# Three row tiles of the first attention's output projection, with their norms, moved between the next tile's quads

## The reference, cut to what matters

```
h = rmsnorm(x, attn_pre_g)
proj = h @ w_in                     # queries, keys, values, gates
o_nsa = nsa_attention(...)          # 8 heads: compressed, selected and window branches
o_swa = swa_attention(...)          # 8 heads: window of 128 keys, with sinks
mix = concatenate([o_nsa, o_swa]) @ w_o
x = x + rmsnorm(mix, attn_post_g)
h = rmsnorm(x, mlp_pre_g)
gu = h @ w_gate_up                  # then the convolution, GELU, w_down
```

## Time and profile before

| | |
|---|---|
| median of three runs | 1631.01 us |
| the profiled execution's own time | 1629.0 us |
| its span in the trace | 1627.7 us |
| TensorE busy | 1505.7 us, 93% |
| VectorE, ScalarE, GpSimd busy | 69%, 38%, 44% |

### The profile page before, as it was taken

The page is one execution under the profiler, slowest core; times in us unless marked ns, Lnnn a source line. Parts: engine busy times, 40 slices in busy tenths (PEclk is TensorE's granted clock), DMA queues, the critical chain, the costliest instruction groups (busy, mean ns, idle before and its releaser), DMA issues.

```text
span 1627.7 us, 22505 instructions
## 1 busy us (share of the span) xinstructions
PE 1505.7 (93%) x8093; PEld 1291.1 (79%) x8093; DVE 1126.9 (69%) x2372; ACT 616.4 (38%) x1536; POOL 712.0 (44%) x668
## 2 busy tenths in 40 slices
PE   5998777999999999999999999999997999999997
PEld 4787455788888787877798899889885787899886
DVE  7746566457767769638867677767777588777764
ACT  3324556231221220113544554454455355344431
POOL 6855000347867748685444034303435114524430
PEclk8997799999999999999999999999999999999999
DMA  6622000424434336553311011101102321111121
GB/s 185 198 88 91 1 1 1 143 89 146 142 121 138 118 107 227 184 185 114 124 53 40 14 53 53 33 20 52 53 27 78 121 99 52 58 47 40 65 91 52
DMA packets 115887, 142.61 MB, mean 88 GB/s; under 512 B 11048, under 2 KB 75200, under 8 KB 115776
## 3 DMA queue, kind: packets, MB, share of 16 engines
q1 hardware_dynamic: 89968, 91.77, 18.2%
q10 hardware_dynamic: 25808, 49.40, 9.1%
HBM read 132.74 MB, written 8.40 MB: 87 GB/s over the span
## 4 chain that ended last, share of the span: by engine, by line
PE 65%; DVE 16%; ACT 8%; POOL 5%; issue 4%; DMA 1%; ACTq 0%; SPq 0%; DVEq 0%; POOLq 0%
PE ps L510 17%; PE ps L512 17%; PE ps L511 17%; POOL w_lo L499 3%; PE ps L1486 2%; PE ps L1290 2%; ACT p L2130 2%; POOL w_hi L497 2%; DVE st L2911 2%; PE ps L924 1%; PE ps L982 1%; PE ps L948 1%; DVE p L2579 1%; PE ps L1500 1%; PE ps L902 1%
## 5 line engine op out<-in xcount | busy, mean ns | idle before, releaser
L497 POOL TENSOR_SCALAR w_hi<-w_raw 128x512 fp32r<-128x512 f32 x308 | 236.5, 768 | 640.5 <-PE ps L512 484.9
L499 POOL TENSOR_TENSOR w_lo<-w_raw,w_hi 128x512 fp32r<-128x512 f32 x316 | 443.8, 1405 | 29.8 <-ACT w_hi L1676 4.1
L510 PE MATMUL ps<-w_hi,h_hi 128*128 128x384 f32 (+2 forms) x768 | 278.0, 362 | 8.1 <-POOL w_lo L499 2.9
L512 PE MATMUL ps<-w_hi,h_lo 128*128 128x384 f32 (+2 forms) x768 | 265.6, 346 | 0.0
L511 PE MATMUL ps<-w_lo,h_hi 128*128 128x384 f32 (+2 forms) x768 | 265.0, 345 | 0.0
L510 PE MATMUL ps<-h_hi,w_hi 128*128 128x512 f32 (+1 forms) x616 | 243.9, 396 | 6.3 <-DVE h_lo L2405 2.6
L512 PE MATMUL ps<-h_hi,w_lo 128*128 128x512 f32 (+1 forms) x616 | 236.7, 384 | 0.0
L511 PE MATMUL ps<-h_lo,w_hi 128*128 128x512 f32 (+1 forms) x616 | 236.5, 384 | 0.0
L2629 DVE SCALAR_TENSOR_TENSOR mod_acc<-mod_piece,csil,mod_acc 128x512 f32<-128x512 f32 x140 | 158.6, 1172 | 19.8 <-DMA mod_piece<-in_ada_w 16.0
L510 PEld LDWEIGHTS ps<-w_hi,h_hi 128*128 128x128 f32 x768 | 147.2, 192 | 20.4 <-POOL w_lo L499 4.3
L511 PEld LDWEIGHTS ps<-w_lo,h_hi 128*128 128x128 f32 x768 | 147.4, 192 | 8.3 <-issue 0.5
(11 more groups left out here) (337 smaller groups left out, 2999.4 us busy)
## 6 DMA issues: line engine op xcount, KB each, us to landing
mod_piece<-in_ada_w ACTq DMA_DIRECT2D x96, 256.0 KB, 3.0
w_raw<-in_w_gate_up SPq DMA_DIRECT2D x88, 256.0 KB, 3.1
w_raw<-in_a_w_in SPq DMA_DIRECT2D x128, 128.0 KB, 2.2
w_raw<-in_w_down SPq DMA_DIRECT2D x22, 512.0 KB, 4.5
w_raw<-in_b_w_in SPq DMA_DIRECT2D x20, 512.0 KB, 3.6
w_raw<-in_w_out SPq DMA_DIRECT2D x16, 512.0 KB, 3.9
w_raw<-in_w_in SPq DMA_DIRECT2D x8, 512.0 KB, 4.1
w_raw<-in_w_o SPq DMA_DIRECT2D x8, 512.0 KB, 3.9
```

The source lines that it names most:

```text
L497: pool.tensor_scalar(hi[:, e, :], raw[:, e, :], 1.0, 0.0, ALU.mult, ALU.add).then_inc(*s["pool_step"].up())
L499: m = pool.tensor_tensor(lo[:, e, :], raw[:, e, :], hi[:, e, :], ALU.subtract)
L510: pe.matmul(out, a[0], b[0], start=start, stop=False)
L512: return pe.matmul(out, a[1], b[0], start=False, stop=stop)
```

## The change

What is computed stays the same. The halves of the projection of tiles 0, 1 and 2 are cut into feature chunks of three matmuls and spread over steps of the next tile's quads (`O_STEPS`), all six of them into bank 3, one after the other. So the scores have three banks left, 0 to 2. ScalarE takes the squares of a finished half and copies it out of bank 3, behind the step after its last chunk. VectorE does the norm of a whole tile behind quads 12, 18 and 22 (`Y1_BEHIND`), ScalarE the squares of the summed rows of tiles 0 and 1 at steps 27 and 47. Tile 0's rows are turned at steps 47 and 51. After the quads are left: the turns of tiles 1 and 2, the projection and norms of tile 3, and the first half of the first gated product, now feature chunk by feature chunk over all four banks.

Two rules of the order change with it. Slots are scored to three behind the quad's last instead of four, but at least to the end of the next quad (`scored_behind`). Values are issued one pair at a time instead of two, and turned chunks have eight places instead of twelve. The rows `x2` and `y1` now lie where the queries of the same tile were, in pieces of 128 columns; their loads and stores move with them.

```diff
-SLOTS_T, SLOTS_T_EARLY = 12, 5
+SLOTS_T, SLOTS_T_EARLY = 8, 5
...
+    def x2(self, t):
+        return self.q_rows[:, 0:8, t * P:(t + 1) * P]
+    def y1(self, t):
+        return self.q_rows[:, 8:16, t * P:(t + 1) * P]
...
 def slots_behind(qs, n):
 
-    total = qs[-1].slots[-1] + 1
-    return range(0, 4) if n < 0 else [i + 4 for i in qs[n].slots if i + 4 < total]
+    if n < 0:
+        return range(0, SCORE_BANKS)
+    return range(scored_behind(qs, n - 1) + 1, scored_behind(qs, n) + 1)
+def scored_behind(qs, n):
+    last = qs[-1].slots[-1]
+    if n < 0:
+        return SCORE_BANKS - 1
+    if n + 1 == len(qs):
+        return last
+    return min(last, max(qs[n].slots[-1] + SCORE_BANKS, qs[n + 1].slots[-1]))
...
-VALUES_AT_ONCE = 2
+VALUES_AT_ONCE = 1
+SCORE_BANKS = 3
+O_STEPS = {(0, 0): range(12, 17), (0, 1): range(18, 23), (1, 0): range(27, 32), (1, 1): range(33, 39), (2, 0): range(45, 51), (2, 1): range(52, 58)}
+H2_STEPS = {47: (0, 0), 51: (0, 1)}
+X2_LOADS = {8: 0, 22: 1, 40: 2}
+ROW_SQUARES = {27: 0, 47: 1}
+Y1_BEHIND = {12: 0, 18: 1, 22: 2}
+H2_BEHIND = {19: (0, 0), 20: (0, 1)}
+def out_chunks(step):
+    parts = []
+    for (t, nh), steps in O_STEPS.items():
+        parts += [(t, nh, c) for c in range(KD) if steps[c * len(steps) // KD] == step]
+    return parts
+def halves_behind(step):
+    return [part for part, steps in O_STEPS.items() if steps[-1] + 1 == step]
...
-    if slot >= 4:
-        pe.wait_ge(*s["b_exped"].at(slot - 4))
+    if slot >= SCORE_BANKS:
+        pe.wait_ge(*s["b_exped"].at(slot - SCORE_BANKS))
...
-        out, x = k.ps[:, slot % 4, c0:c0 + q.w], k.qst[:, q.head0 + e, q.t * P:(q.t + 1) * P]
+        out, x = k.ps[:, slot % SCORE_BANKS, c0:c0 + q.w], k.qst[:, q.head0 + e, q.t * P:(q.t + 1) * P]
...
+    if first and q.kind == 2 and q.t == TX - 1:
+        pe.wait_ge(*s["turn_lo"].at(("h2", 0, 1)))
...
-            for part in values.pop(turn_number(qs, q.n, i), ()):
+            step = turn_number(qs, q.n, i)
+            for part in values.pop(step, ()):
                 pe_pair_values(k, pe, qs, *part)
+            for part in out_chunks(step):
+                pe_project_chunk(k, pe, *part)
+            if step in H2_STEPS:
+                pe_turn_rows(k, pe, *H2_STEPS[step], 7)
...
+def pe_project_chunk(k, pe, t, nh, c):
+    s = k.sig
+    if c == 0 and nh == 0:
+        pe.wait_ge(*s["o_lo"].at((t, 2)))
+    if c == 0 and t < TX - 1:
+        if nh == 1:
+            pe.wait_ge(*s["y_half"].at(("o", t, 0)))
+        elif t > 0:
+            pe.wait_ge(*s["y_half"].at(("o", t - 1, 1)))
+    if c == 0 and t == TX - 1:
+        if nh == 0:
+            pe.wait_ge(*s["b_exped"].at(quads()[-1].slots[-1]))
+        else:
+            pe.wait_ge(*s["y_half"].at(("o", t - 1, 1)))
+    if c % 2 == 0:
+        pe.wait_ge(*split_at(k, ("o", nh), c))
+    bank = 3 if t < TX - 1 else 2 + nh
+    m = three(pe, k.ps[:, bank, :], [x[:, c, t * P:(t + 1) * P] for x in k.h1], k.hl(("o", nh), c, 0, 512), c == 0, c == KD - 1)
+    if c == KD - 1:
+        m.then_inc(*s["prod"].up(("o", t, nh)))
+def pe_turn_rows(k, pe, t, g, bank):
+    s = k.sig
+    pe.wait_ge(*s["dve_step"].at(("out1", t)))
+    if (t, g) == (0, 1):
+        pe.wait_ge(*s["turn_lo"].at(("h2", 0, 0)))
+    if t == 1:
+        pe.wait_ge(*s["b_pt"].at(turn_number(quads(), len(quads()), 0) - 2 + g))
+    if t == 2:
+        pe.wait_ge(*s["o_lo"].at((TX - 1, 2)))
+    if t == 3:
+        pe.wait_ge(*s["turn_lo"].at(("h2", 2, g)))
+    for j in range(4):
+        m = pe.transpose(k.ps[:, bank, j * P:(j + 1) * P], k.y1(t)[:, 4 * g + j, :], k.ident[:, :])
+    m.then_inc(*s["turn_ps"].up(("h2", t, g)))
...
-    pe_first_cols(k, pe, 3, 0, range(FIRST_TURN_AT, KD))
+    for g in range(2):
+        pe_turn_rows(k, pe, 1, g, 4 + g)
+    for nh in range(2):
+        for c in range(KD):
+            pe_project_chunk(k, pe, TX - 1, nh, c)
+        if nh == 0:
+            for g in range(2):
+                pe_turn_rows(k, pe, 2, g, 6 + g)
+    pe.wait_ge(*k.sig["turn_lo"].at(("h2", 1, 1)))
+    for c in range(KD):
+        if c == FIRST_TURN_AT:
+            for g in range(2):
+                pe_turn_rows(k, pe, 3, g, 6 + g)
+        for i in range(4):
+            pe_first_cols(k, pe, i, 0, range(c, c + 1))
...
+            step = turn_number(qs, q.n, i)
+            for o in plan.pop(step, ()):
                 outputs(o)
+            if step == 1:
+                act.dma_start(k.post1[:, :], k.row(k.ins["attn_post_g"])).then_inc(*s["post1_in"].up("all", 16))
+            if step in X2_LOADS:
+                act_row_load(k, act, qs, X2_LOADS[step])
+            for part in halves_behind(step):
+                act_out_half(k, act, *part)
+            if step - 1 in H2_STEPS:
+                act_rows_turned(k, act, *H2_STEPS[step - 1], 7)
+            if step in ROW_SQUARES:
+                act_row_squares(k, act, ROW_SQUARES[step])
     for step in sorted(plan):
         for o in plan[step]:
             outputs(o)
+def act_row_load(k, act, qs, t):
+    s = k.sig
+    act.wait_ge(*s["b_scored"].at([q for q in qs if q.t == t and q.kind == 1][-1].slots[-1]))
+    act.dma_start(k.x2(t), k.xin()[:, t, :].rearrange("p (c n) -> p c n", n=P)).then_inc(*s[f"x2_in{t}"].up("x", 16))
+def act_out_half(k, act, t, nh):
+    s, half, out = k.sig, k.y1(t)[:, 4 * nh:4 * nh + 4, :], k.chunks(3)
+    act.wait_ge(*s["prod"].at(("o", t, nh)))
+    act.activation(half, out, ACT.Square, accum_out=k.halves[:, nh, 2 * t:2 * t + 1]).then_inc(*s["act_step"].up())
+    act.wait_ge(*s["act_step"].now())
+    act.activation(half, out, ACT.Copy).then_inc(*s["y_half"].up(("o", t, nh)))
+def act_rows_turned(k, act, t, g, bank):
+    act_turn(k, act, k.h1[0][:, 4 * g:4 * g + 4, t * P:(t + 1) * P], bank, ("h2", t, g), gain=k.gx[:, 1, 4 * g:4 * g + 4])
+def act_row_squares(k, act, t):
+    s = k.sig
+    act.wait_ge(*s["added"].at(("y1", t)))
+    act.dma_start(k.x_dram[:, t, :].rearrange("p (c n) -> p c n", n=P), k.x2(t)).then_inc(*s["x_out"].up(("1", t), 16))
+    act.activation(k.y1(t), k.x2(t), ACT.Square, accum_out=k.halves[:, 0, 2 * t + 3:2 * t + 4]).then_inc(*s["sq"].up(("y1", "x", t)))
...
-            if step <= turn_number(qs, q.n, 0):
+            if step <= turn_number(qs, q.n, len(q.chunks) - 1):
                 for o in plan.pop(step):
                     outputs(o)
+        if q.n in H2_BEHIND:
+            dve_rows_turned(k, dve, *H2_BEHIND[q.n], 7)
+        if q.n in Y1_BEHIND:
+            dve_add_out(k, dve, Y1_BEHIND[q.n])
...
+def dve_add_out(k, dve, t):
+    s, y, with_row = k.sig, k.y1(t), 0 < t < TX - 1
+    if t < TX - 1:
+        dve.wait_ge(*s["y_half"].at(("o", t, 1)))
+        first = k.halves[:, 0, 2 * t:2 * t + 1]
+        dve.tensor_tensor(first, first, k.halves[:, 1, 2 * t:2 * t + 1], ALU.add).then_inc(*s["dve_step"].up())
+        dve.wait_ge(*s["dve_step"].now())
+    else:
+        dve.wait_ge(*s["sq"].at(("y1", "y", t)))
+    if with_row:
+        dve.wait_ge(*s["sq"].at(("y1", "x", t - 1)))
+    dve_inverse_rms(k, dve, 2 * t, 2 * t + (2 if with_row else 1), ("y1", t))
+    dve.wait_ge(*s["rms"].at(("y1", t)))
+    if with_row:
+        dve_scale_out(k, dve, t - 1)
+    dve.wait_ge(*s["post1_in"].at("all"))
+    dve.wait_ge(*s[f"x2_in{t}"].at("x"))
+    gain = k.post1[:, :].rearrange("p (c n) -> p c n", n=P)
+    for nh in range(2):
+        half = slice(4 * nh, 4 * nh + 4)
+        x = y[:, half, :] if t < TX - 1 else k.chunks(2 + nh)
+        m = dve.scalar_tensor_tensor(y[:, half, :], x, k.stat[:, 1, 2 * t:2 * t + 1], gain[:, half, :], ALU.mult, ALU.mult)
+    m.then_inc(*s["dve_step"].up())
+    dve.wait_ge(*s["dve_step"].now())
+    dve.tensor_tensor(k.x2(t), k.x2(t), y, ALU.add).then_inc(*s["added"].up(("y1", t)))
```

More of the change, by code:

```diff
@@ L188, in lay_memory @@
         self.junk1 = Memory(nc, at_k).tile("junk1", [P, D])
-        late = Memory(nc, at_k)
-        self.x2, self.post1 = late.tile("x2", [P, TX, D]), late.tile("post1", [P, D])
-        assert late.offset <= m.offset
         after_k = m.offset
@@ L203, in lay_memory @@
         self.pt_early, self.pt_late = Memory(nc, at_acc).tile("pt_early", [P, SLOTS_T_EARLY, S]), m.tile("pt_late", [P, SLOTS_T - SLOTS_T_EARLY, S])
+        self.post1 = m.tile("post1", [P, D])
         free.tile("under_pt", [P, 3, S])
@@ L626, in output_steps @@
     return out
-O_BANKS = ((0, 1), (2, 3))
 OUT0_BANKS = ((5, 7), (6, 0), (1, 2))
@@ L1838, in act_project_out @@
 def act_project_out(k, act):
-    s = k.sig
-    last = quads()[-1]
-    act.wait_ge(*s["b_scored"].at(last.slots[-1]))
-    act.dma_start(k.post1[:, :], k.row(k.ins["attn_post_g"])).then_inc(*s["post1_in"].up("all", 16))
-    for t in range(TX):
-        act.dma_start(k.x2[:, t, :], k.xin()[:, t, :]).then_inc(*s[f"x2_in{t}"].up("x", 16))
-    def rows(t):
-        return k.rows1[:, t, :]
-    def turn_out(t):
-        for g in range(2):
```

(30 more changed lines are left out.)

59 lines of the change are left out of this document (14 added, 45 removed).

## The result

| | before | after |
|---|---|---|
| time, median | 1629.55 us | 1659.3 us |
| ratio | 1 | 1.0182 (95%: 1.0165 to 1.0198) |
| profiled execution / span | 1629.0 / 1627.7 us | 1658.2 / 1656.9 us |
| end of the last attention output (P) | 288.9 us | 351.9 us |
| from P to the second half of columns | 61.1 us | 31.8 us |

The forecast was 1634.0, with a range of 1613 to 1650. It had the end right (30.2 us from P) and the quads wrong: they grew by 63 us, not 35. One execution of a later kernel (the one with all three edits) took 8295 us where its others took some 1628; nothing here explains it, and its ratio leaves it out.

A forecast was written before the change was run, and what follows sets the result against it. A chain of hand-overs was taken to bound the quads, TensorE's work the projection. Quad terms summed to 37.0 us, less 2 for the clock, 35 against 30.9 saved at the end: 4 us slower, 1634 us, range 1613 to 1650.

The forecast's parts named there:

- end stretch: From the last attention output to the second half of columns: 61.1 us shrinks to 30.2, giving 30.9 (26 to 36).
- shorter look-ahead: In quads of two slots, the next scale waits for a slot scored behind the first turn: 12.5 us (6 to 18).
- wait for the third bank: In quads of four slots, the fourth slot waits for the first exponential: four rounds, 2.4 us (0 to 5).
- chunks in front of the second turn: In the quads, eight of 48 chunks delay the turn ScalarE waits for: 8 x 0.69 = 5.5 us (0 to 33).
- norms, tile 0's turns, tile 2's norm: In the quads: norms of tiles 0 and 1 10.3 us, tile 0's turns 1.0, tile 2's norm behind quad 23 2.1.
- squares and copies of halves: On ScalarE in the quads, six halves at 1.3 us each, two between exponentials, with three loads: 3.2 us (1 to 10).
- clock: In the quads, more matmuls in between remove some time at the lower clock level: 2 us off (0 to 5).
- values, eight places: In the quads, values one pair at a time and eight places for turned chunks count as nothing.
- the norm comes ahead of that and covers the chunks of these rounds: Behind quads 13 and 19: the norm precedes VectorE's 2.1 us wait; rounds grow 5.1 and 5.2 us, chunks there free.
- the third rival: In rounds with a norm, TensorE hangs at the fourth slot and restarts at lower clock: 14 us more, 1648; 20%.
- the round behind quad 10: From quad 10's scale to quad 11's: 3.65 us before, 7.3 us forecast, so +3.7 by the shorter look-ahead.

The follow-up runs named there:

- the one with all three edits: Changed kernel with chunks behind a quad's last turn, third and fourth slot behind second and third turn, norms in three pieces: 1628.7 us, ratio 1.0.
- the 26 of three banks: Kernel before with three score banks and the changed order of score slots, projection and norms left behind the quads: 1655.1 us; quad 23 26.0 us late.
- the later slots: Changed kernel with the third score slot issued behind the second turn and the fourth behind the third: 1647.1 us, ratio 1.0115.
- On four banks: Kernel before with the changed kernel's shorter look-ahead (three ahead, not four) but its own four score banks: 1649.0 us, ratio 1.0124.
- the form with bank 7: Changed kernel with four banks, only tiles 0 and 1 projected in quads, into bank 7: 1626.9 us; adding tile 0's norm in pieces 1619.9, then three banks 1643.9.

## Why the prediction was wrong

The last attention output came at 351.9 us, where the forecast named 333 as the latest that it could stand. By its own steps, with the forecast and what the runs showed:

| step | forecast | measured |
|---|---|---|
| end stretch | gives 30.9 (26 to 36) | 29.3 |
| shorter look-ahead | 12.5 (6 to 18) | 21 |
| wait for the third bank | 2.4 (0 to 5) | 5 |
| chunks in front of the second turn | 5.5 (0 to 33) | 21, left out |
| norms, tile 0's turns, tile 2's norm | 13.4 | 17, left out (18 by the last output, which tile 2's norm can delay) |
| squares and copies of halves | 3.2 (1 to 10) | not taken alone |
| clock | gives 2 | lost: 0.92 to 0.87 |
| values, eight places | 0 | 0 |

Measured by quad 23's reciprocal; "left out" is what came back when that work was taken out of the quads. Chunks and norms so give 38 us, where chunks, norms and halves together cost 35 (61 less the 26 of three banks): they share a wait. The miss of 28 us in the quads is made up so: 11 for look-ahead and bank (26 for 14.9), 15 for chunks, halves and the norms of tiles 0 and 1 with their turns (35 for 20.0), and the 2 taken off for the clock.

**The step that failed** is the price of the chunks. The forecast counted eight of 48, 5.5 us, and excused the rest as lying behind the third turn or in rounds "that a norm or a shorter look-ahead already lengthens", as if a round that is longer had free time in it. They cost 21 us, spread over ten rounds and more at 1.4 to 2.8 us each, the two with norms (2.1 and 1.4) among them. Behind the last turn of a quad the same chunks cost 15 us less.

For the norms the same thought reads "the norm comes ahead of that and covers the chunks of these rounds". It is true of the work and false of the order. The chunks stand in TensorE's queue behind the fourth slot, and that slot waits for the first exponential, which waits for the least behind the norm. Nothing that was queued behind the slot ran while it stood. So 5.9 us of standing come first and the values and chunks after it, in front of the next turn, at the lower level of the clock. That is the third rival, "the norms cascade", nearly word for word: it was priced at 1648 for rounds over 15 us, and the rounds came out at 17.2, 17.6 and 15.1; the 11 us from there to 1659 are those of look-ahead and bank. That the later slots, without one instruction less, give 12 us back shows it. In these two rounds the standing is more than the chunks: a norm was priced at 5.1 and 5.2 us, and without them, chunks kept, the rounds are 7.0 and 6.3 us shorter.

**The look-ahead was mis-sized** by 9 us and the bank's wait by 3. On four banks the round from quad 22 to 23 grew by 3.6 us (forecast 2.7, with a half's copy in it) and 16 to 17 by 3.4 (3.2), so the forecast named a true cost, though quad 10's round grew by 1.6 and not 3.7. What it did not work out is how far the loss spreads: 11 us before quad 10 in the kernel with pairs of values, and in the form with bank 7, with the values one at a time, only 3.7 there but 6.8 in the round from 22 to 23 alone. Whether the values make that difference was not tested. And the upper bound of 18 was drawn round the estimate, not from a row.

**The clock** was given the wrong sign. The forecast took 2 us off because more matmuls would stand in the gaps. In the stretch from 180 to 287.5 it is 0.87, that is 28 us at 1.2 GHz instead of 17. The added matmuls did not lower it. With three banks and no chunk it is 0.84, and with the chunks left out and the norms kept:

```profile
180.00:287.50 107.50, 68.36 (x322) 40.88 (x320) 63.58 (x217) 56.95 (x164) 0.00 (x0) 0.82 0.07 20
```

So the chunks raised it, as the forecast had it, from a level that the shorter look-ahead had lowered, and that fall is what the forecast left out. Where the gaps were in fact filled, in the form with bank 7, it is 1.00. The Trainium skill (TensorE: Matmul & The Clock Gate, "What's actually happening") says that the default state is throttled and activity releases it; the traces agree on both sides, 0.84 with idle gaps lengthened and 1.00 with them filled.

**Right** were the end (31.8 us for 30.2, with 5.85 us for the root beside the split and 2.3 without it, 358.82 - 352.97 and 372.22 - 369.90), the values and places at nothing, and the round behind quad 10 in direction: 9.4 us for 7.3.

**What stays open:** how much ScalarE's squares and copies of halves cost by themselves, and what gives 4.5 us back behind the second half of columns.

## What to carry to other kernels

A bank or a buffer taken from a pipeline for new work has a price of its own, whether the new work fits or not (here 27 us alone, 24 beside 22 us of chunks): try the shallower pipeline alone first. Work put beside a long instruction of another engine is covered only if it stands in its own queue ahead of the instruction that waits; behind it, it is added. Look for a resource that is free part of the time (here the bank of the third kind of output) before taking one that is in use, and put an engine's long work right ahead of where it waits, in pieces about as long as the wait (here 1.2 to 2.4 us for waits of 2.1, which gave 7 us).
